# Two modulation weight slots moved out of the ring, a small turn moved between two products, and another VectorE order in the second projection

## The reference, cut to what matters

```
def conv_ffn(h, w_up, conv_w, conv_b, w_down, rows):        # end of block one
    u = h @ w_up                                            # 1024 -> 2 x 2816
    u = conv2d_grid(u, conv_w, rows) + conv_b               # 3x3, one filter per channel, 8 x 64 grid
    gate, val = jnp.split(u, 2, axis=-1)
    return (jax.nn.silu(gate) * val) @ w_down               # 2816 -> 1024

m_lat = jax.nn.silu(c) @ w_mod[l] + b_mod[l]                # block two: 6 x 1024 numbers
sh1, sc1, g1, sh2, sc2, g2 = jnp.split(m_lat[:, None, :], 6, axis=-1)
m_ctx = jax.nn.silu(c_ctx) @ w_mod[l] + b_mod[l]
h = modulate_2(rmsnorm(x, norm_mix[l]), sh1, sc1)
proj = h @ w_in[l]
```

## Time and profile before

| | |
|---|---|
| median of three timed runs | 1937.88 us |
| the profiled execution's own time | 1932.17 us |
| its span in the profile | 1930.3 us |
| mean granted TensorE clock | 0.962 |
| TensorE busy | 1763.5 us, 91% |
| VectorE busy | 999.7 us, 52% |
| ScalarE busy | 414.2 us, 21% |
| moved by DMA | 379.94 MB, mean 197 GB/s |

### The profile page before, as it was taken

The page is one execution under the profiler, slowest core; times in us unless marked ns, Lnnn a source line. Parts: engine busy times, 40 slices in busy tenths (PEclk is TensorE's granted clock), DMA queues, the critical chain, the costliest instruction groups (busy, mean ns, idle before and its releaser), DMA issues. The chain is left out here.

```text
span 1930.3 us, 28062 instructions
## 1 busy us (share of the span) xinstructions
PE 1763.5 (91%) x11854; PEld 1056.2 (55%) x11854; DVE 999.7 (52%) x1671; ACT 414.2 (21%) x797; POOL 162.9 (8%) x223
## 2 busy tenths in 40 slices
PE   7999998889999999999998999899979889888876
PEld 3554487777444444588887888654443333332322
DVE  1776884566698989832488889643040100000013
ACT  4223544341201010101211111540031101111101
POOL 0000027510000000000020111100010000000000
PEclk9999998999999999999999999899979899899899
DMA  8462034223322222322385422303569999999995
GB/s 351 175 229 99 17 93 96 53 102 101 135 81 72 80 75 78 148 90 90 126 315 208 131 88 88 115 23 114 218 224 411 427 424 428 425 426 425 426 426 242
DMA packets 80529, 379.94 MB, mean 197 GB/s; under 512 B 34464, under 2 KB 37536, under 8 KB 54672
## 3 DMA queue, kind: packets, MB, share of 16 engines
q1 hardware_dynamic: 70000, 350.03, 47.0%
q0 software_dynamic: 7104, 26.68, 3.8%
q10 hardware_dynamic: 3296, 1.38, 0.3%
HBM read 364.09 MB, written 19.92 MB: 199 GB/s over the span
## 5 line engine op out<-in xcount | busy, mean ns | idle before, releaser
L3652 PE MATMUL psum<-mem 128*64 128x512 f32 x1504 | 355.6, 629 | 33.9 <-DMA mem<-in_w_upe 17.6
L2404 PE MATMUL psum<-mem 128*128 128x512 f32 x704 | 302.9, 591 | 0.6 <-ACT mem L377 0.6
L3652 PEld LDWEIGHTS psum<-mem 128*64 128x64 f32 x1504 | 115.2, 144 | 254.3 <-issue 247.7
L2513 DVE SCALAR_TENSOR_TENSOR mem<-mem 128x512 f32<-128x512 f32 x352 | 236.9, 745 | 0.0
L2404 PEld LDWEIGHTS psum<-mem 128*128 128x128 f32 x704 | 132.9, 189 | 170.2 <-issue 169.0
L2760 PE MATMUL psum<-mem 128*128 128x256 f32 x896 | 197.3, 381 | 6.6 <-DVE mem L2941 6.0
L2760 PEld LDWEIGHTS psum<-mem 128*128 128x128 f32 x896 | 169.9, 190 | 33.9 <-DVE mem L2941 5.7
L1680 PE MATMUL psum<-mem 128*128 128x256 f32 x616 | 138.2, 384 | 1.3 <-DVE mem L1729 0.7
L3723 DVE TENSOR_TENSOR mem<-mem,psum 128x512 f32<-128x512 f32 x16 | 11.0, 688 | 244.2 <-issue 211.8
L1680 PEld LDWEIGHTS psum<-mem 128*128 128x128 f32 x616 | 117.3, 192 | 21.0 <-issue 3.9
L698 PE MATMUL psum<-mem 128*128 128x512 f32 (+1 forms) x336 | 119.0, 513 | 0.0
(11 more groups left out here) (423 smaller groups left out, 2206.3 us busy)
## 6 DMA issues: line engine op xcount, KB each, us to landing
mem<-in_w_upe SPq DMA_DIRECT2D x30, 2048.0 KB, 25.2
mem<-in_w_gate SPq DMA_DIRECT2D x29, 2048.0 KB, 28.5
mem<-in_w_downe SPq DMA_DIRECT2D x27, 2048.0 KB, 30.3
mem<-in_ada SPq DMA_DIRECT2D x32, 1024.0 KB, 6.1
mem<-in_w_up SPq DMA_DIRECT2D x22, 1024.0 KB, 4.9
mem<-in_ada POOLq DMA_DIRECT2D x16, 1024.0 KB, 6.3
mem<-in_w_in_g SPq DMA_DIRECT2D x12, 1024.0 KB, 4.9
mem<-in_w_down SPq DMA_DIRECT2D x16, 704.0 KB, 4.3
```

The costliest lines, as they stand in the source:

```text
L2404: last = pe.matmul(k.bank[2 * (m % 3) + h2][:, :], w[:, kt, h2], h[:, kt], start=kt == 0, stop=kt == KD - 1)
L2513: ins = dve.scalar_tensor_tensor(out=a, in0=src, scalar=w, in1=a, op0=MUL, op1=ADD)
L3652: last = pe.matmul(bank[halves[h], :], xs[:, kt, halves[h]], pair[h][0][:, kt, cols], start=kt == 0, stop=kt == tiles - 1, skip_group_chec ...
```

## The change

- Of the eight early modulation slots the last two (6 and 7) leave the ring. Two places of their own, in memory unused in this stage, receive them by `load_apart`, which SyncE issues after the ring tile of up product 7. So the ring holds slots 3 to 5 ahead of the first down weights, and the first down tile takes the slot of the last up tile.
- TensorE turns the modulation rows between p1 and p2 of the first pair; it waits there for the last padded copy. Before, the turn stood behind p3.
- ScalarE copies the fourth bank of rows ahead of the last silu.
- VectorE waits for all row products before it makes s1 of pair 0, since s1 overwrites the apart places.
- In the second projection VectorE does `c11` of pair 0 ahead of `make_s` of pair 1, and late slot 9 stays behind that. Slots 10 and 11 go to pairs 0 and 1 (one each, behind c22), 12 and 13 to pair 2, 14 and 15 to pair 3. Before, pairs 0 to 2 had two each.

```diff
@@ order_of_use, constants
+MOD_APART = 6
-    for g in range(MOD_EARLY, 8):
+    for g in range(MOD_EARLY, MOD_APART):
         k.put("ada2", g)
@@ SecondMod
-        for g in range(8):
+        for g in range(MOD_APART):
             k.freed[k.number("ada2", g)] = [(self.mm, g + 1)]
+
+    def load_apart(self, sp):
+        for w, g in zip(self.apart, range(MOD_APART, 8)):
+            sp.dma_start(w, self.k.d["ada2"][g]).then_inc(self.apart_landed, 16)
...
+        if g < MOD_APART:
+            n = k.number("ada2", g)
+            k.weights_ready(pe, n)
+            w = k.slot(n)
+        else:
+            pe.wait_ge(self.apart_landed, 16 * (8 - MOD_APART))
+            w = self.apart[g - MOD_APART]
@@ ffn_stage, SyncE
+            k.send_weights(sp, k.number("w_up", 8))
+            mod.load_apart(sp)
             k.send_weights(sp, k.number("w_down", 4))
@@ ffn_stage, TensorE
             down.do_p1(pe, 0)
+            pe.wait_ge(s["padded"], KF)
+            mod.turn(pe)
             pe.wait_ge(mod.rows_done, 2)
             pe.wait_ge(s["hidden"], KF)
             down.do_p2(pe, 0)
-            pe.wait_ge(s["padded"], KF)
             down.do_p3(pe, 0)
-            mod.turn(pe)
             down.do_p5(pe, 0)
@@ ffn_stage, ScalarE
                 if m == KF:
                     mod.take_rows(act, 1)
                     mod.take_rows(act, 2)
+                    mod.take_rows(act, 3)
...
-            mod.take_rows(act, 3)
             warm_root(k, act)
@@ ffn_stage, VectorE
             product(KF - 1)
+            dve.wait_ge(mod.mm, 8)
             down.make_s1(dve, 0)
@@ SecondProjection.vector
+        self.c11(dve, 0)
         self.make_s(dve, 1)
         self.late.slot(dve, self.LATE_FIRST - 1)
-        self.c11(dve, 0)
@@ SecondProjection.fill
-        if p < 3:
-            self.late.slot(dve, self.LATE_FIRST + 2 * p + part)
+        if p < 2 and part == 1:
+            self.late.slot(dve, self.LATE_FIRST + p)
+        if 2 <= p < 4:
+            self.late.slot(dve, self.LATE_FIRST + 2 * p - 2 + part)
```

More of the change, by code:

```diff
@@ L1958, with __init__ @@
     BANKS, TURNED = (5, 7, 2, 3), 1
-    def __init__(self, k, rows, c32):
-        self.k, self.rows, self.c32 = k, rows, c32
+    def __init__(self, k, rows, c32, apart):
+        self.k, self.rows, self.c32, self.apart = k, rows, c32, apart
+        self.apart_landed = k.sem("mod2_apart_landed")
         self.mm, self.rows_done, self.turned, self.added, self.ready = (k.sem("mod2_" + n) for n in ("mm", "rows", "turned", "added", "c32"))
-        for g in range(8):
+        for g in range(MOD_APART):
             k.freed[k.number("ada2", g)] = [(self.mm, g + 1)]
+    def load_apart(self, sp):
+        for w, g in zip(self.apart, range(MOD_APART, 8)):
+            sp.dma_start(w, self.k.d["ada2"][g]).then_inc(self.apart_landed, 16)
     def rows_by_product(self, pe, g):
         k = self.k
-        n = k.number("ada2", g)
-        k.weights_ready(pe, n)
-        w = k.slot(n).rearrange("p (k m) -> p k m", k=KD)
+        if g < MOD_APART:
[5 more added lines that the diff above has]
+            w = self.apart[g - MOD_APART]
+        w = w.rearrange("p (k m) -> p k m", k=KD)
         if g == 0:
@@ L2624, in block_one @@
     norm2, gains2 = Norm(k, "norm2", 22528, k.bank[4], k.bank[6]), k.small[:, 16:24]
-    mod = SecondMod(k, k.at(25600, 2048), k.at(25088, 256).rearrange("p (k m) -> p k m", k=KD))
+    mod = SecondMod(k, k.at(25600, 2048), k.at(25088, 256).rearrange("p (k m) -> p k m", k=KD), [k.at(17408 + SLOT * i, SLOT) for i in range(2)])
     quarters_of = mixed_at[:, 0:8:2], mixed_at[:, 1:8:2], gated[:, :, 0:256], gated[:, :, 256:512]
```

## The result

The changed kernel took 1920.69 us in the median of six runs (1919.16 to 1925.92); six runs of the kernel before gave 1936.99. The ratio is 0.9937, 95% interval 0.9917 to 0.9957, 12.2 us of 1937; the two medians are 16.3 us apart. The forecast was 1930.2 us, range 1925.0 to 1936.5, faster with 0.67.

A forecast was written before the change was run, and what follows sets the result against it. TensorE was taken to set the pace behind the up projection until the experts, where DMA bounds. Gains of 5.35 us (up to down) and 2.3 (second projection) sum to 7.65, so 1930.2 against 1937.88, range 1925 to 1936.5.

The forecast's parts named there:

- What bounds, and what shifts: TensorE sets the pace behind the up projection until the experts; time saved on it there moves all that follows forward.
- Rivals 2 to 4: Late first down tile, 1933.2, chance 0.12; projection gives gain back, 1936, 0.10; gather behind weights in experts, 1946, 0.05.
- Rival 1: The clock stays up both from up to down and in the second projection: gain 10.85 us, 1927.0, chance 0.12.
- Up to down: Part 1, from the up loop's end to the end of p6: 825.5 against 830.85, a gain of 5.35 us.
- the turn under the wait for the hidden activations: Up to down: the turn, 3.76 us, ends at 803.2, before p2 can start at 804.55, so it costs nothing.
- s1 without its DMA wait: Up to down: VectorE's s1, which waited 1.38 us for its last down tile, starts at 804.5, 1.3 us earlier.
- the clock, taken at 1.6 us: Up to down: a clock fall after p1 and the turn costs 1.6 us, bounds nothing to 3.3.
- Second projection: Part 2, VectorE's new order: TensorE gains 2.3 us, bounds 1.5 to 3.9.
- The 3.90 us of the shortened wait: Second projection: p3 starts at 1024.17 against 1028.07, 3.90 us gained at full clock, with 4.0 us of idle left.
- The 1.6 us for the clock: Second projection: the remaining idle brings a clock fall costing 1.6 us, bounds 0 and 2.04 plus 0.4.
- Sum: Both parts: 5.35 + 2.3 = 7.65 us off the profiled 1932.17, and 1930.2 against the median 1937.88.
- gains of 5.2 to 10.4 us: The main forecast's own range over both parts, given as 1927.5 to 1932.9, with chance 0.61.

The follow-up runs named there:

- c22 ahead: The changed kernel with c22 of pair 0 also ahead of late slot 9, slots 10 and 11 in pair 1: 1918.34 us, ratio 0.9917 to the kernel before.
- after, third: The changed kernel, unedited, profiled and timed a third time: 1925.44 us (12 runs), ratio 0.9960 to the kernel before.
- part 2 alone: The kernel before with only the second projection's VectorE order changed: 1929.49 us (12 runs), ratio 0.9977.
- after: The changed kernel's first profile, 1923.15 us; its first series took 1920.69 us (six runs), ratio 0.9937 to the kernel before.
- part 1 alone: The changed kernel with the second projection's old VectorE order put back: 1931.64 us (12 runs), ratio 0.9988 to the kernel before.

## Why the prediction was right and where it was wrong

**What bounds, and what shifts.** Right. The 133.04 us between the two places are the same in all profiles, and the start of the experts moved with the rest. Rivals 2 to 4 didn't come: no late down tile (the wait ahead of p1 was 0.49 us), no new wait for VectorE in pairs 2 and 3, and the experts took 587.4 to 589.9 us, within what they took before (586.2 and 588.5) and with other kernels. Rival 1, a clock that stays up, came in the projection in two profiles of three, and in up to down in none.

**Up to down, 5.35 us forecast, 4.84 measured** (5.3, 4.6, 4.8 and 4.8 in the four other profiles that have it). The steps came as told: five slots in 4.53 us, p1 right behind, the turn under the wait for the hidden activations, s1 without its DMA wait. The mis-sized term is the clock, taken at 1.6 us. p2, p3, p5 and p6 took 21.44 us for 19.36, 2.1 us, and that is the whole miss of 0.5. The turn was slowed by 0.9 us to 4.63 too, but the wait behind it hid this: p2 started 14.69 us behind the first row product (790.43 to 805.12), where 14.67 was forecast. The gain lay within the bounds given (3.7 to 6.95).

**Second projection, 2.3 us forecast, 4.14 measured.** The 3.90 us of the shortened wait came (3.78 left for 4.0 expected). The 1.6 us for the clock didn't, in this profile; with the wait 0.2 us shorter than expected, that is the 1.8 us of the miss in the profiled run. Over the five profiles with this order it cost nothing twice and 1.7 to 2.3 us three times, so the term varies from one profile to the next, 5.7/5 = 1.1 us on average. The prediction also took the old order to lose nothing behind its waits, since the low clock ended within them. That was so in the profile that it read; in three of five with that order the same products lost 2.2 to 2.5 us, 1.4 on average. So on average the clock's loss is nearly the same on both sides, and the new order gains its 3.9 us and some tenths.

**Sum.** 7.65 us forecast, 8.7 with an uncertainty of 1.7 over all 118 runs. The size of the change was right within that, and so was the mechanism but for where the clock's losses fall. A slip in the prediction: gains of 5.2 to 10.4 us off 1937.88 give 1927.5 to 1932.7, not 1932.9, and the two upper bounds add up to 10.85, not 10.4.

**The step that failed** is the last one of the sum, as I put it: "so against 1937.88 the forecast is 1930.2", with a range of 1925 to 1936.5. I took three runs as the kernel's time and laid nearly all of the range into the change. The other 90 runs show what three can't: over all 93 the kernel before has a median of 1933.3, from 1926.0 to 1946.5; 1937.88 was 4.6 us above it. The first six runs of the changed kernel, 1920.69, were 3.3 us below its median over all 25, 1924.01. So the 9.5 us between forecast and measurement are 4.6 from the level of the kernel before, 3.3 from the spread of the first six runs of the changed one, and 1.6 from the change itself (9.3 us between the two large medians, 7.65 forecast). The row that could have warned me stood in my own table: the profiled execution was 5.7 us under the median, and I let it pass as an offset.

The range failed with it. It had rival 1, 1927.0, and 2 us for a run's spread at its low end. From the level of all 93 runs, 1933.3, rival 1 gives 1922.4, and six runs of the changed kernel can lie 3.3 us off its level; the low end had to be near 1919. Taking the profiled 1932.17 as a fourth run would have moved the median by only 0.5 us and would not have saved it.

**Where that spread comes from** the first column of the table shows: identical code ahead of the change starts the up loop anywhere between 486.0 and 494.2. The last of the small 64x64 products of the scan (L1227 before) starts at 406.5 us in the fastest and 413.6 in the slowest of the thirteen profiles, while that stage itself starts within 3.1 us in all (240.9 to 244.0 for the first of L1149). The granted clock falls there one to five times, at other places each time, but the number of falls doesn't order the profiles: "c22 ahead" has three and ends at 413.0, "after, third" four and ends at 406.9. So what makes the spread stays open. The experts add some 5 us (586.2 to 591.5).

The Trainium skill ("TensorE: Matmul & The Clock Gate", Part 1) says that the gate's timing is free-running and isn't reset when a kernel starts. The profiles fit this and don't prove it: with one and the same wait of 3.8 us the clock fell in "part 2 alone" and not in "after".

## What to carry to other kernels

Two edits can each be worth nothing and together five us of a stage (in the timed runs of part 1 alone 2.3 us were left of it, with an interval from nothing to 4.8): one that frees an engine earlier needs work to put into the opened gap, and one that moves work off the path needs a gap to move it into. Test them together before dropping either. Where an engine waits for one addition behind a long filler, put the addition first, and look at the whole row of fillers that can slide back into later slack. And before a range is drawn around a change of half a percent, ask how far the baseline itself is known: single runs of this kernel spread by 3.8 us (the standard deviation of the 93), and the median of the first three was 4.6 us off, half of what the change is worth.

## What the runs showed of the hardware that I had not expected

- The clock fell in the middle of the turn, 2.4 us after its start, with TensorE shown 1.00 busy (802 to 803). In eight of the ten profiles where the sixteen products of two columns stand as one block it fell within the block. In the other two the block ran through at full clock and the fall came 0.4 us behind its end (part 2 alone) and 1.7 us behind it, after 0.89 us of idle (part 1 alone). Woven between products of 256 columns they held the clock in two profiles of three.
- A wait of 3.8 to 4.2 us on TensorE brought the clock down in three profiles of five. Where it did, the next 28 products took 50.4 to 51.0 us instead of 48.70. With the old order, a wait of 5.1 to 5.3 us brought it down in five of five, and the same products lost nothing twice and 2.2 to 2.5 us three times. The price of such an idle stretch is thus its length plus nothing or some 2 us.
- Code that is the same in all thirteen kernels took 164.5 to 170.5 us in a stage of many small products (first of L1149 to last of L1227).
